# Modulation rows repeated by DMAs inside SBUF, a ninth weight chunk in a home used once, x1 rows and initial sums in expert 1

## What is computed

```python
mod = (jnp.einsum('bd,de->be', jax.nn.silu(c), w_ada) + b_ada)[:, None, :]
sh1, sc1, gt1, sh2, sc2, gt2 = jnp.split(mod, 6, axis=-1)
...
x = x + gt1 * (merged @ w_o)
h2 = _rmsnorm(x, g_ffn) * (1.0 + sc2) + sh2
x = x + gt2 * _moe(h2, w_router, b_router, w_gate_up, b_gate_up, w_down, b_down)
```

## Time and profile before

| | us |
|---|---|
| median of 3 runs | 1392.13 |
| lowest, highest | 1390.81, 1394.26 |
| the profiled execution | 1390.95 |
| its span (first to last instruction) | 1389.1 |
| PE busy | 1353.6 (97%) |
| VectorE, ScalarE, GpSimd busy | 501.1, 219.8, 67.6 |
| moved by DMA | 487.81 MB, mean 351 GB/s |

### The profile page before, as it was taken

One profiled execution on the slowest core, in us unless ns is written; L12 is line 12 of the kernel. 1 busy time (PEld: TensorE's weight loads), 2 busy tenths in 40 slices (PEclk: granted clock), 3 DMA queues, 4 the chain that ended last, 5 costly groups with the idle time before them and its releaser, 6 DMA issues.

```text
span 1389.1 us, 17563 instructions
## 1 busy us (share of the span) xinstructions
PE 1353.6 (97%) x6742; PEld 549.9 (40%) x6742; DVE 501.1 (36%) x1081; ACT 219.8 (16%) x407; POOL 67.6 (5%) x65
## 2 busy tenths in 40 slices
PE   8999999999999999999999999999999999999996
PEld 4544555555456333333333333333333333333332
DVE  3245887853124322332233222422223222233225
ACT  2111232121022211111111111111111111111102
POOL 1003402220001000000000000000000000000000
PEclk9999999999999999999999999999999999999998
DMA  9424354387877799999999999999999999999994
GB/s 387 161 98 166 122 128 159 105 311 272 345 314 307 280 428 428 428 426 428 428 430 427 428 428 430 428 428 427 430 428 428 427 430 429 427 428 429 430 425 185
DMA packets 62302, 487.81 MB, mean 351 GB/s; under 512 B 8327, under 2 KB 30407, under 8 KB 33836
## 3 DMA queue, kind: packets, MB, share of 16 engines
q1 hardware_dynamic: 59948, 482.43, 84.4%
q0 software_dynamic: 1152, 4.19, 0.8%
q10 hardware_dynamic: 1152, 0.52, 0.1%
HBM read 483.01 MB, written 4.08 MB: 351 GB/s over the span
## 4 chain that ended last, share of the span: by engine, by line
PE 76%; DMA 18%; DVE 3%; ACT 1%; issue 0%; SPq 0%; DVEq 0%
PE ps L1759 23%; PE ps L1786 12%; DMA z<-in_w_gate_up 10%; DMA ring<-in_w_gate_up 7%; PE ps L1068 6%; PE ps L1069 5%; PE ps L1680 5%; PE ps L1083 3%; PE ps L1731 3%; PE ps L1551 3%; PE ps L1745 2%; PE ps L1046 2%; PE ps L1735 1%; PE ps L1393 1%; PE ps L1382 1%; DMA ring<-in_w_mid 1%
## 5 line engine op out<-in xcount | busy, mean ns | idle before, releaser
L1759 PE MATMUL ps<-ring,z 128*64 128x512 f32 x1552 | 343.7, 594 | 9.8 <-DMA ring<-in_w_gate_up 9.1
L2455 DVE TENSOR_SCALAR actT<-ps 128x512 f32<-128x512 f32 x32 | 22.1, 692 | 589.6 <-PE ps L1759 589.6
L1759 PEld LDWEIGHTS ps<-ring,z 128*64 128x64 f32 x1552 | 108.5, 137 | 239.4 <-issue 217.6
L1786 PE MATMUL ps<-ring,z 128*64 128x512 f32 x752 | 167.7, 594 | 0.0
L1068 PE MATMUL ps<-ring,actT 128*128 128x512 f32 (+1 forms) x200 | 102.4, 594 | 1.3 <-DVE actT L1941 1.1
L1069 PE MATMUL ps<-ring,actT 128*128 128x512 f32 (+1 forms) x200 | 100.3, 583 | 0.0
L1786 PEld LDWEIGHTS ps<-ring,z 128*64 128x64 f32 x752 | 52.5, 137 | 109.9 <-issue 109.1
L1680 PE MATMUL ps<-z,actT 128*64 128x512 f32 x384 | 89.1, 597 | 0.2 <-DVE actT L2371 0.2
L1731 PE MATMUL ps<-z,aT 128*128 128x512 f32 x120 | 62.0, 619 | 0.0
L1759 PE MATMUL ps<-z 128*64 128x512 f32 x256 | 57.9, 594 | 3.0 <-DMA z<-in_w_gate_up 3.0
L2400 DVE TENSOR_TENSOR xr<-xr,z 128x512 f32<-128x512 f32 (+1 forms) x75 | 59.8, 797 | 2.6
(11 more groups left out here) (370 smaller groups left out, 1305.1 us busy)
## 6 DMA issues: line engine op xcount, KB each, us to landing
ring<-in_w_gate_up SPq DMA_DIRECT2D x97, 2048.0 KB, 27.1
ring<-in_w_down SPq DMA_DIRECT2D x47, 2048.0 KB, 29.7
z<-in_w_gate_up SPq DMA_DIRECT2D x16, 2048.0 KB, 27.6
more_w<-in_w_gate_up SPq DMA_DIRECT2D x15, 2048.0 KB, 26.4
ring<-in_w_in SPq DMA_DIRECT2D x11, 2048.0 KB, 7.6
more_w<-in_w_down SPq DMA_DIRECT2D x9, 2048.0 KB, 30.6
ring<-in_w_mid SPq DMA_DIRECT2D x8, 2048.0 KB, 9.3
z<-in_w_down SPq DMA_DIRECT2D x8, 2048.0 KB, 33.0
```

What stands on the lines that cost most here:

```text
L1759: done = nc.tensor.matmul(bank(q // 2)[64 * (q % 2):64 * (q % 2) + 64, :], lhs, homes[home][4 * (k % 2) + q], start=False, stop=k == 7)
L1786: done = nc.tensor.matmul(bank(2)[64 * q:64 * q + 64, :], lhs, homes[home][2 * (k % 4) + q], start=k == 0, stop=k == 7)
```

## The change

`spread_rows` leaves PE. The bias of rows 64 to 72 and 96 to 104 (once for each of the nine rows) is loaded early into `bias_rows`, after GpSimd has zeroed them; `modulation_out` adds it where it copied. Four DMAs from SBUF to SBUF for each of `sh2` and `gt2` repeat the rows: one row 128 times for each half of the prompt's, eight rows 8 times each for each half of the sample's. They are issued by SyncE, those of `sh2` before the output weights, those of `gt2` after the router weights. The matmuls of `spread_rows`, the ScalarE copies behind them and their semaphores go; waits on them become waits on the DMAs.

Chunk 8 (expert 1, third of gate/up) gets a home of its own, made of `xr` and a part of `z`, used once. It is issued once the spread rows are there, its last quarter after the transposes of the h2 rows (`rows_tr` 15). All later chunks move by one home.

All `rows_of(x1c, ...)` go into expert 1, since `xr` now holds weights until then: tiles 2 and 0 between its gate/up and `x_rows`, tile 1 after that. The three initial sums follow: tiles 0 and 2 between the halves of expert 1's `down`, tile 1 after it. Further, the GpSimd add of `sh2p` is cut into four pieces, the step `nmr` is moved behind the first picks, and some buffers change place.

The core of the diff:

```diff
+        bias_rows = [xr[:, 1024 + 512 * i:1536 + 512 * i] for i in range(2)]
+        homes.append([xr[:, BANK * i:BANK * (i + 1)] for i in range(6)] + [ysb[1][:, BANK * i:BANK * (i + 1)] for i in range(2)])
...
             def load_bias_rows(i, signal):
-                sp.wait_ge(tb_mm, 1 + i)
                 for h in range(2):
                     at = (6 + 4 * i + h) * BANK
-                    sp.dma_start(mod_rows[i][73 + 32 * h:74 + 32 * h, :], a["b_ada"][:, at:at + BANK]).then_inc(signal, 16)
+                    sp.dma_start(bias_rows[i][64 + 32 * h:73 + 32 * h, :].unsqueeze(1),
+                                 a["b_ada"][:, at:at + BANK].partition_broadcast(1 + DB)).then_inc(signal, 16)
+
+            def spread_rows(i, prompt, sample, signal):
+
+                sp.wait_ge(partb_done, 1 + i)
+                for h in range(2):
+                    c = slice(BANK * h, BANK * (h + 1))
+                    rows = mod_rows[i][64 + 32 * h:73 + 32 * h, :]
+                    sp.dma_start(prompt[:, c], rows[0:1].unsqueeze(1).broadcast_to([1, P, BANK])).then_inc(signal, 16)
+                    sp.dma_start(sample[0:NS, c], rows[1:1 + DB].unsqueeze(1).broadcast_to([DB, DS, BANK])).then_inc(signal, 16)
...
             load_modulation(20, 2)
+            sp.wait_ge(z_zeroed, 3)
+            load_bias_rows(0, part_here)
+            load_bias_rows(1, g_here)
...
             load_modulation(24, 6)
+            sp.wait_ge(yb_mm, 1)
+            spread_rows(0, sh2p, sh2s, sh2_here)
             load_tile(26, in_tile("w_out", 0))
             load_tile(27, in_tile("w_out", 1))
             sp.wait_ge(tile_done, 26)
             sp.dma_start(wr, a["w_router"].rearrange("(k p) e -> p k e", p=P)).then_inc(rw_here, 16)
-            load_bias_rows(1, g_here)
+            spread_rows(1, gt2p, gt2s, gt2_here)
...
-            sp.wait_ge(g2_mm, 2)
+            sp.wait_ge(wo_mm, 3)
             chunk(1, 1, 7)
...
-            for n in range(SLOTS, 24):
-                sp.wait_ge(chunk_used, n - 7)
-                chunk(n // 6, n % 6, n)
+            w = a["w_gate_up"][1:2, 512:768, :].rearrange("a (p i) n -> (a p) (i n)", i=2)
+            sp.wait_ge(sh2_here, 16 * (DB + 4))
+            sp.wait_ge(gt2_here, 128)
+            sp.dma_start(xr[:, :], w[:, 0:6 * BANK]).then_inc(c_here, 16)
+            sp.wait_ge(rows_tr, 15)
+            sp.dma_start(ysb[1], w[:, 6 * BANK:8 * BANK]).then_inc(c_here, 16)
+
+            for n in range(ONCE + 1, 24):
+                sp.wait_ge(chunk_used, n - 8 if n <= 2 * SLOTS else n - 7)
+                chunk(n // 6, n % 6, n - 1)
...
+            nc.gpsimd.memset(xr[:, 1024:2048], 0.0).then_inc(z_zeroed, 1)
...
-            nc.gpsimd.tensor_tensor(h2[:, 1, :], h2[:, 1, :], sh2p, ALU.add).then_inc(pool_sum, 1)
+            for c in range(4):
+                q = slice(256 * c, 256 * (c + 1))
+                last = nc.gpsimd.tensor_tensor(h2[:, 1, q], h2[:, 1, q], sh2p[:, q], ALU.add)
+            last.then_inc(pool_sum, 1)
...
                 for k in range(KT):
+                    if c == 0 and k == KT // 2:
+                        pe.wait_ge(rows_done, 12)
...
             def expert(p, s, buf, at, turns, first, last, sums):
...
-                if s == 0 and sums:
+                if s and sums:
                     rows_of(x1c, 2, 4)
+                    pe.wait_ge(rows_done, 13)
+                    rows_of(x1c, 0, 6)
...
                 elif sums:
-                    start_sum(1)
+                    pe.wait_ge(rows_done, 15)
+                    rows_of(x1c, 1, 6)
...
-                elif sums:
-                    start_sum(2 if s else 0)
-
-                down(n, chunks[4:6], first and not s)
+                elif sums and s == 0:
+                    pe.wait_ge(gT_done, 1)
+
+                if sums and s:
+                    down(n, chunks[4:6], False, (0, 4))
+                    start_sum(0)
+                    start_sum(2)
+                    down(n, chunks[4:6], False, (4, 8))
+                    start_sum(1)
+                else:
+                    down(n, chunks[4:6], first and not s)
...
             def modulation_out(i):
                 dve.wait_ge(tile_done, 22 + 4 * i)
-                nc.vector.tensor_copy(mod_rows[i], bank(7 - i)).then_inc(partb_done, 1)
+                dve.wait_ge((part_here, g_here)[i], (48, 64)[i])
+                nc.vector.tensor_tensor(mod_rows[i], bank(7 - i), bias_rows[i], ALU.add).then_inc(partb_done, 1)
...
-            nc.vector.tensor_scalar(nmr, m8r[:, :, 0], -1.0, None, ALU.mult).then_inc(m0_done, 1)
-            dve.wait_ge(part_done, 5)
+            dve.wait_ge(sh2_here, 16 * (DB + 4))
             dve.wait_ge(rows_tr, 14)
             nc.vector.scalar_tensor_tensor(h2[:, 0, :], bank(0, 2), st[:, 11:12], sh2p, ALU.mult, ALU.add).then_inc(h2_done, 1)
```

More of the change, by code:

```diff
@@ L88, in constants @@
     r = np.arange(P)
[L90 to L91 removed]
+    t["selp"] = np.tile((r == 0)[:, None], (1, P))
+    t["sels"] = r[:, None] == 1 + np.arange(NS)[None, :] // DS
     i = np.arange(P)
@@ L518, in _, with chunk @@
             sp.dma_start(wr, a["w_router"].rearrange("(k p) e -> p k e", p=P)).then_inc(rw_here, 16)
-            load_bias_rows(1, g_here)
-            def chunk(e, k, n):
-                slot = n % SLOTS
+            spread_rows(1, gt2p, gt2s, gt2_here)
+            def chunk(e, k, turn):
+                slot = turn % SLOTS
                 if k < 4:
@@ L556, in _ @@
                 sp.wait_ge(chunk_used, n - 7)
-                chunk(NE - 2 + s, k, n)
+                chunk(NE - 2 + s, k, n - 1)
             sp.wait_ge(chunk_used, 6 * NE - 7)
@@ L580, in _ @@
                             sp.wait_ge(chunk_used, i * 24 + (6 * NE + 6 * j + k - 7))
-                            chunk(e, k, 6 * j + k)
+                            chunk(e, k, 6 * j + k - 1)
                 store_result(3)
@@ L939, in expert @@
                 nc.scalar.activation(sgm, gb, ACT.Sigmoid, scale=1.702).then_inc(sig_done, 1)
-                if sums and half == 0:
+                if sums and half:
                     x1_rows_out(2)
+                    x1_rows_out(0)
                 if not last:
@@ L950, in expert @@
                     xt_out(n + 1)
+                if sums and half:
+                    x1_rows_out(1)
                 slots_out(buf, half, n * 6 + 6)
@@ L1499, in modulation_transposes @@
                 last.then_inc(tb_mm, 1)
-            def spread_rows(i, signal):
-                for name in ("selp", "sels"):
-                    if i == 0 and name == "sels":
-                        pe.wait_ge(rows_done, 12)
-                    for k in range(2):
-                        rows = slice(64 + 32 * k, 96 + 32 * k)
-                        out = bank(4)[NS * k:NS * k + NS, :] if name == "sels" else bank(k)
-                        last = nc.tensor.matmul(out, const(name)[rows], mod_rows[i][rows], start=True, stop=True)
-                    last.then_inc(signal, 1)
             pe.wait_ge(side_here[0], 48)
@@ L1773, in activation_transposes, with down @@
                 done.then_inc(at_tr, 1)
-            def down(n, chunks, first=False):
-                pe.wait_ge(at_done, n + 1)
-                if not first:
-                    pe.wait_ge(y_done, n)
-                for k in range(8):
+            def down(n, chunks, first=False, steps=(0, 8)):
+                if steps[0] == 0:
+                    pe.wait_ge(at_done, n + 1)
+                    if not first:
+                        pe.wait_ge(y_done, n)
+                for k in range(*steps):
                     home, here = chunks[k // 4]
@@ L1790, in down, with landing @@
                         done.then_inc(chunk_used, 1)
-            def landing(m, turns):
-                slot = m % SLOTS
-                return slot, turns * 16 + (BEFORE[slot] + 16 * (m // SLOTS + 1))
+            def landing(m, turns, beginning=False):
+                if beginning and m == ONCE:
+                    return SLOTS, 64
+                turn = m if beginning and m < ONCE else m - 1
+                slot = turn % SLOTS
+                return slot, turns * 16 + (BEFORE[slot] + 16 * (turn // SLOTS + 1))
             def expert(p, s, buf, at, turns, first, last, sums):
                 n = p * 2 + s
-                chunks = [landing(6 * (at + s) + k, turns) for k in range(6)]
+                chunks = [landing(6 * (at + s) + k, turns, sums) for k in range(6)]
                 gate_up(n, chunks[0:4], first and not s)
@@ L2298, in _ @@
                     dve.wait_ge(tb_mm, 1)
-                    for half, (dst, at) in enumerate(((gt1T, 2 * KT), (sh2T, 3 * KT))):
-                        nc.vector.tensor_tensor(by_chunk(dst), columns_of(half), spread(badaT[:, at:at + KT]),
-                                                ALU.add).then_inc(col_done, 1)
+                    nc.vector.tensor_tensor(by_chunk(gt1T), columns_of(0), spread(badaT[:, 2 * KT:3 * KT]), ALU.add).then_inc(col_done, 1)
```

(5 more changed lines are left out.)

85 lines of the change are left out of this document (30 added, 55 removed).

## The result

| | before | after |
|---|---|---|
| median, us (4 runs each) | 1391.7 (1390.8 to 1394.3) | 1418.07 (1416.2 to 1418.3) |
| ratio, with its 95% interval | | 1.0186 (1.0173 to 1.0199) |
| span of the profiled execution, us | 1389.1 | 1416.3 |
| mean granted clock of TensorE | | 0.986 |

The changed kernel is 26.4 us slower. The forecast was 4.4 us faster, and its range ended at 1403.

A forecast was written before the change was run, and what follows sets the result against it. The chunk stream was taken to bound the kernel. First gate/up 3.6 us earlier, less 1.0 in expert 1, moved the bound from 1363.5 to chunk 24's 1359.1: 4.4 us off the median 1392.13 gave 1387.7, range 1384.7 to 1403.

The forecast's parts named there:

- What bounds the kernel: Whole kernel: the stream of 192 weight chunks sets the end, by a waiting chunk's issue time plus chunks left times 4.90.
- chunk 24: Expert weight stream: this chunk, issued at used 17, becomes the bound after the change, at 1359.1 against 1363.5 before.
- Spreading by DMA: Before output weights and before first expert chunks: each spread writes 0.79 MB, taken as 4 us, all hidden in idle transfer time.
- the first rival: Both spreads: a repeated row is read slowly, 26.8 GB/s, 21 us a spread; +9 us, 1401; chance 0.22.
- s: At the first output tile: PE's standing time for late output weights, D - 13 us.
- D: Length of one spread in us; stream ends at 1344.4 + s + D, deciding from 13; sign turns at about 16.5.
- Row spreading off TensorE: Between output projection tiles: two groups of 8 matmuls go, gaining 0.5 (router weights awaited) and 2.06 us.
- GpSimd add in four pieces: Before the position matmuls: VectorE's comparison is held by one piece, not the whole 2.35 us add; gain 1.0 us.
- x1 rows and initial sums into expert 1: Experts 0 and 1: frees 4.2 us before used 5, 4.97 less 1.0 before used 11; loses 1.0 before used 17.
- used 5: Expert weight stream: the moment when PE has finished 5 chunks, which released chunk 12 before and chunk 13 after the change.
- Ninth chunk: Chunks 9 to 16 wait one use less; gains 0.6 us alone, while chunk 24 is no nearer.
- The sum: Terms 0.5 + 2.06 + 1.0 bring first gate/up 3.6 us earlier, to about 451.4; kernel 4.4 us earlier, 1387.7.

The follow-up runs named there:

- the 128-partition kernel: Changed kernel, but the four transfers repeating a prompt row read all 128 partitions of the modulation tile instead of one partition 128 times: 1389.2 us, ratio 0.998.
- the one with TensorE's spreading: Changed kernel with the old spreading by TensorE matmuls and ScalarE copies put back, the rest of the change kept: 1392.1 us, ratio 1.0.
- the bias kernel: Changed kernel, but the gate/up bias load is issued from ScalarE's queue instead of SyncE's, at the same point of the program: 1405.5 us, ratio 1.0093.
- the last three kernels: Two-hop kernel with bias rows' tile cleared later (1388.95 us); that without the ninth chunk's head start (1388.74); that with router weights before the second output-weight tile (1388.0).
- the two-hop kernels: Changed kernel with each prompt row sent to 32 partitions, then each of these to four, from ScalarE's queue: 1390.8 us, ratio 0.999; later edits build on it.
- the kernel with the router weights ahead: Two-hop kernel with late clearing of the bias rows' tile, router weights issued ahead of the second tile of output weights: 1388.0 us, ratio 0.997.
- the two kernels that read pairs: Changed kernel, each prompt transfer reading two partitions 64 times each: 64 with 68, 1404.7 us, ratio 1.01; 64 with 96, 1422.0 us, ratio 1.0208.

## Why the prediction was wrong, point by point

**What bounds the kernel** was right: the stream, judged by issue time plus chunks left times 4.90. The formula puts the changed kernel 26.2 us later (26.4 measured), the 128-partition kernel 2.8 earlier (3.2 measured) and the one with TensorE's spreading 0.2 later (0.2 earlier measured). It was 3 us short for the bias kernel, where the beginning of the stream took over, and it gives the last three kernels 2.6 to 3.5 us where 1.2 to 3.9 were measured, so elsewhere it is good to about 2 us. That **chunk 24** would be the bound was right in every trace but the bias kernel's.

**Spreading by DMA** is the step that failed. It took 4 us for a spread, by the rate of a repeated row of HBM (205 GB/s). That row shows how fast repeated rows can be written, but the spread reads inside SBUF, and the row says nothing of that. The dear price, 26.8 GB/s, stood under the first rival with a chance of 0.22. Measured: 27 GB/s in the prompt transfers and 21.3 and 23.4 us for the spreads, the rival's 21. The nearest row by name was the wrong one; the property that differed, one source partition, had no row at all in the trace of before, so the cheap end was no likelier than the dear one.

**The first rival** had the mechanism and most of its parts, but 9 us for a loss of 26. Its parts: output weights near 405.5, measured 410.9; TensorE stands 8 us, measured 10.4; router weights near 411, measured 416.3; first spread from 378 to 399, measured 383.8 to 405.1; second from 411 to 432, measured 412.7 to 436.1. It then let the stream set the end (432 + 0.6 + 192 x 4.90 = 1373.4), which is what the bias kernel shows (1375.4 by its own trace, 1405.5 us measured against the rival's 1401). What it lacked was the queue behind the second spread. The gate/up bias, 256 KB, is issued behind seven chunks on SyncE's queue; with the chunks 32 us late it lands 24 us after its issue, at 475. The prediction followed the backlog to the output weights, the router weights and the first chunks, but not to the load that TensorE needs before its first gate/up. And it had no term for the clock: 0.50 after each wait, 2.6 + 0.9 + 2.85 us. Two of its sums are off as well. By its own terms chunk 24 (1359.1 + s) stays the bound until D = 14.7, not 13. And the about 1403 us beside an estimated 23 us for a spread is what its formula gives for 22; for 23 it gives 1344.4 + 10 + 23 = 1377.4, which is 1405.

**Row spreading off TensorE**: forecast 2.56 us (0.5 + 2.06). The kernel with 128 source partitions and the one with TensorE's spreading differ by this alone: their chunk 24 lies 2.99 us apart, the medians 2.9. Of the 2.99, 0.8 are there already ahead of the first group (372.25 against 373.03 at the same matmuls), so some 2.2 are the spreading's. Right within 0.4. The wait for the router weights, forecast at 1.5, is 2.2.

**GpSimd add in four pieces**: the comparison was to take 0.8 us and took 0.21, and the gain of 1.0 on the way to the first gate/up was about right: in the 128-partition kernel the first x_rows start 3.7 us after the sample tile's h2 transposes begin, where it was 5.0 before. The answer to the earlier trace rows:

```profile
456.74 2.78 POOL L711 TENSOR_TENSOR z<-z 128x256 f32<-128x256 f32 x4 [7.77 <-ACT z L903]
457.35 0.21 DVE L2365 TENSOR_SCALAR z<-z 128x96 f32<-128x96 f32 x1
```

**x1 rows and initial sums into expert 1**: forecast, from the first gate/up's start, 1.0 later at chunk 24, 4.0 earlier at chunk 18 and 4.2 earlier for used 5. The 128-partition trace: 84.9 us to chunk 24 instead of 83.5 (+1.4), 51.7 instead of 55.3 to chunk 18 (-3.6), 22.4 instead of 26.5 to used 5 (-4.1). Right. It was not undone by itself on the chip, so what it is worth for the time is argued from the traces only.

**Ninth chunk**: 0.6 alone, nothing with the rest. The run without its head start has 0.2 us less, within the noise: nothing.

**The sum**: first gate/up at 451.4, measured 452.6 in the 128-partition kernel, with the late copy (1.2 us at this point in the kernel before), and 451.5 and 452.4 in two of the two-hop kernels with the copy on time. 1387.7 forecast with cheap spreads, 1389.2 measured for the kernel that has them. The sum held for everything except the price that it rested on.

## What to carry to other kernels

Before a broadcast moves from an engine to a DMA, ask from how many source partitions it reads, and not only how many it writes; if the trace has no such read, follow the dear end of its price through everything queued behind it, to the last small load that an engine will wait for. A slow transfer costs the queue behind it, not its own length: here two spreads of 21.3 and 23.4 us cost 26 us, half of it at a 256 KB load issued 77 us after the first one. Spreading in two hops, from a queue with nothing urgent on it, takes the loss away. Of the gain, 0.3% showed only with the router weights issued earlier as well.

## What the runs showed of the hardware that was not expected

- Reads of one partition move 27 GB/s at a DMA share of 0.87 to 0.91 (14 to 15 engines' time); reads of 64 and 96 move 26 and those of 64 and 68 move 53, both at the time of two engines.
- Such a read of one partition keeps the engines occupied (share 0.9). From a queue of its own it still stretches a 128 KB load from 7.9 to 23.3 us.
- With the queue full of slow packets, an issue holds SyncE for up to 10.82 us (L451), where the first spread's two took 0.74 and 0.66. In the two kernels that read pairs, whose packets go to two engines' time, the first spread's already take 5.8 us and 5.7 or 7.45.
- Reading two partitions 64 times each took two engines' time (share 0.13), and with 64 and 96 these two then moved their share of the output weights alone for some 10 us (408 to 418).
- TensorE's granted clock fell without a wait on record: in the kernel with the router weights ahead it was 0.57 in 505 to 508, with TensorE busy for all of 503 to 510, and 16 matmuls took 5.35 us instead of 3.65.
- The VectorE copy near 306 comes 2.1 us late in one trace of the kernel before and not in the other, and their times are 1391.07 and 1390.95.
